# First tile of the first mixing phase read into SBUF within the projection; one identity table for all three phases

## The chip, the cores and the metric

The kernel runs on one core of one Trainium2 chip. The time is the device time of one execution in microseconds (us), from start to end of the program, and the figure used is the median of several executions. Lower is better.

The engines are named as in the profile: PE is the matrix engine (PEld is its weight load), DVE the vector engine, ACT the scalar engine, POOL the general engine, SP the engine that only issues transfers. SPq and ACTq are the transfers that SP and ACT issue; each of the two has a DMA queue of its own (q1 is SP's, q10 is ACT's).

## The reference

One inference step of a two-layer decoder trunk, for a prompt of 2048 tokens and for 8 samples of 8 tokens, width 1024, all in float32:

```
for l in range(2):
    mod = silu(c) @ w_ada[l] + b_ada[l];  shift, scale, gate = split(mod, 3)
    h = rms_norm(x, g_pre[l]) * (1 + scale) + shift
    y, states = mixer_ab(h, ...) if l == 0 else mixer_c(h, ...)
    x = x + gate * rms_norm(y, g_post[l])

mixer_ab: gq,gk,gv,gz,glr, rq,rk,rv,rz = split(h @ w_in)      # 3088 columns
    log_a = log_sigmoid(glr @ w_gate_up + b_gate) / 16        # 4 gated heads
    q_r, k_r = rotary(rq), rotary(rk)                         # 4 retention heads
    o, S = chunked_gated_linear_attn(q, k, v, log_g, s0)      # S_t = g_t S_{t-1} + k_t v_t
    y = (normalised per head(o) * silu(z)) @ w_out
mixer_c:  a gated delta rule with a width-4 convolution on q, k, v
```

## The kernel before

The program is four phases, one after the other. Each phase is a block with one instruction list per engine, and the engines meet at a barrier where a phase ends (`Phase.end`). Between phases, large intermediate results go through DRAM.

1. **inab** (`phase_in_ab`, the first 658 us): the product `h @ w_in` of layer 0. The tokens are taken in four blocks of 512 and a fifth with the 64 sample tokens. Each float32 product is three half-precision matmuls (line 613). Before it, layer 0's conditioning (`Cond`) is computed, with the weight `w_ada`, and the first block is normalised and transposed with the identity table. q and k leave to the DRAM array `qk0`, v to `v0`, z to `z0` and the decays to `dec0`.
2. **mixab** (`phase_mix_ab`, to about 1059 us): the recurrence over 16 tiles of 128 tokens and then the samples. A tile on PE is: transpose k with the identity (line 1675), scores (1685), outputs (1696, 1700), key-values (1709), then the output projection (1117). DVE masks the scores with the table `incl` (1540), decays the state (1549), takes statistics (1557) and gates.
3. **inc** (`phase_in_c`): layer 1's input projection, whose first instructions on PE transpose the convolution weights, which SP has loaded as rows (line 1872), with the identity (2141).
4. **mixc** (`phase_mix_c`): layer 1's recurrence. The change doesn't touch it.

What sets the order around the change:

- **Tables.** Constants (identity, masks, selectors, decays) stand side by side in one DRAM array, in the order `TABLE_ORDER`. `load_tables` (line 172) issues one transfer for each name. Phase inab loads three (`ident`, `sel`, `sel_s`) as SP's third to fifth transfers and seven more after the `w_ada` loads; mixab loads seven; inc loads three. The tables of a phase are in that phase's own SBUF, so the identity is loaded again in each.
- **Waits on tables.** PE's list begins with a wait for them in inab (`first_in`, line 1010), in mixab (`tab_in`, line 1668) and in inc (line 2136); in mixab and inc it is for all tables of the phase. DVE's list in mixab begins with the same wait (1529) and one for POOL's memsets (`init`, 1530, signalled by line 1439, the last of five).
- **Tiles in mixab.** SP's list loads tile 0 (four transfers: q and k, v, z, decays; lines 1370 to 1374), then the tables, then tile 1, then the residual rows of two tiles, the gate, two gain vectors `gn` and `cT`. The rooms for tiles are two of each, used in turn; tile 2 is loaded into the first (`turn(0, ...)`, line 1405) once tile 0 has been mixed.
- **Operand rooms in inab.** The normalised input of a block of 512 tokens stands in one of two rooms of 128 partitions by 4096 floats. Blocks 1 and 3 use the room `h` of phase inab; the fifth block uses a room in `y`. So `h` is not read after block 3. In mixab and inc a room of the same size, `raw_next`, is allocated outside the phases; mixab writes it only near its end.
- **SP in inab's last part.** SP stores a block's results as they come (`outputs`). Between block 3's stores and those of the fifth block it issues the load of rotation angles for the latter (`rot_load`, line 774). The phase ends when the last stores of v and z have landed (line 785).

Of the kernel before, what the change touches and what calls it, by code (L numbers as in the profile page):

```python
# [23 lines left out]
P = 128  # L24
# [165 lines left out]
def width(names):  # L190
    return sum(TABLE[n][1] for n in names)
# [426 lines left out]
def phase_in_ab(nc, io, modT, seq):  # L618
# [9 lines left out]
    first_names = ["ident", "sel", "sel_s"]  # L628
    names = ["swap", "reset", "reset_s", "dec", "dec_s", "retd", "retd_s"]
    tab = ph.sb("tab", [P, width(first_names + names)])  # L630
    tv = table_views(tab, first_names + names)
# [41 lines left out]
    prep = Prep(nc, ph, 0, io["x_prompt"], io["x_sample"], modT, tv["ident"], nt, pst, io["keep32"])  # L673
# [35 lines left out]
    def _(sp):  # L709
        sp.dma_start(c9[0:1, :], io["c_prompt"]).then_inc(c_in, 16)  # L710
        sp.dma_start(c9[1:C9, :], io["c_sample"]).then_inc(c_in, 16)
        load_tables(sp, first_in, tab, first_names, io["table"])
# [5 lines left out]
        load_tables(sp, tab_in, tab[:, width(first_names):], names, io["table"])  # L718
# [205 lines left out]
    def _(dve):  # L924
# [13 lines left out]
        dve.wait_ge(tab_in, 16 * len(names))  # L938
# [70 lines left out]
    def _(pe):  # L1009
        pe.wait_ge(first_in, 16 * len(first_names))  # L1010
# [11 lines left out]
        pe.wait_ge(tab_in, 16 * len(names))  # L1022
# [269 lines left out]
def phase_mix_ab(nc, io, seq):  # L1292
# [4 lines left out]
    io["raw_next"] = io["keep"].enter_context(nc.sbuf_tensor("raw_next", [P, KT, BLK], F32))  # L1297
# [4 lines left out]
    tv = table_views(tab, names)  # L1302
# [4 lines left out]
    dec = [ph.sb(f"dec{i}", [P, 8]) for i in range(2)]  # L1307
    ktok = ph.sb("ktok", [P, PAIRS, P])
# [14 lines left out]
    tile_in = [s("tile_in0"), s("tile_in1")]  # L1323
    init, within = s("init"), s("within")
# [54 lines left out]
    def _(sp):  # L1379
        load_tile(sp, 0, 0, P)  # L1380
# [7 lines left out]
        sp.dma_start(cT[:].rearrange("p k c -> p (k c)"), io["cT"]).then_inc(cT_in, 16)  # L1388

# [15 lines left out]
        turn(0, 0, 0, P, P)  # L1405
# [122 lines left out]
    def _(dve):  # L1528
        dve.wait_ge(tab_in, 16 * len(names))
# [77 lines left out]
        for t in range(4):  # L1607
# [3 lines left out]
            tile(t, t % 2, t // 2)  # L1611
# [55 lines left out]
    def _(pe):  # L1667
        pe.wait_ge(tab_in, 16 * len(names))
# [65 lines left out]
        for t in range(2):  # L1734
            tile(t, t, 0)
# [65 lines left out]
def phase_in_c(nc, io, modT, seq):  # L1801
# [3 lines left out]
    names = ["ident", "incl", "incl_s"]  # L1805
    tab = ph.sb("tab", [P, width(names)])
    tv = table_views(tab, names)
# [327 lines left out]
    def _(pe):  # L2135
        pe.wait_ge(tab_in, 16 * len(names))
# [93 lines left out]

        pe.wait_ge(g_ready, 1)
# [1076 lines left out]
```

## Time and profile before

| | |
|---|---|
| median of 3 runs | 2683.37 us (2681.66 to 2688.16) |
| the profiled execution | 2690.28 us, its span 2688.5 us |
| PE busy | 2488.4 us, 93% of the span |
| DVE, ACT, POOL busy | 49%, 35%, 30% |
| mean granted clock of PE | 0.966 |

The span runs from the first to the last instruction of one execution, taken by the hardware profiler; all positions below are in us from its start. A granted clock of 1.00 is 2.4 GHz, one of 0.50 is 1.2 GHz. A timeline row shows start, duration, engine, line, operation, tiles written and read, how many instructions it merges, and in brackets how long the engine had been idle before it and what released it. For a row that merges several instructions the duration reaches from the first to the last.

### The profile page before, as it was taken

How to read it: one execution, taken by the hardware profiler on the slowest of the kernel's cores; microseconds unless marked ns; L12 is line 12 of the kernel's file. 1: busy time of each engine (PE TensorE's matmuls, PEld its weight loads, DVE VectorE, ACT ScalarE, POOL GpSimd, SP SyncE). 2: the span in 40 equal slices, each digit the busy share in tenths (PEclk: the TensorE clock that was granted, in tenths of full speed). 3: DMA queues.
4: the chain of work that ended last, by engine and by line, in shares of the span. 5: the costliest groups of instructions: out<-in, count | busy, mean ns of one | idle time of the engine just before them, and what ended most of it. 6: DMA issues, size and time to landing. Idle time of an engine off the chain costs nothing. (4 is left out here: it accounts for less than half of the span.)

```text
span 2688.5 us, 53779 instructions
## 1 busy us (share of the span) xinstructions
PE 2488.4 (93%) x20987; PEld 1504.2 (56%) x21052; DVE 1321.5 (49%) x2927; ACT 929.0 (35%) x2666; POOL 798.8 (30%) x848
## 2 busy tenths in 40 slices
PE   6999999997899986998999999994899999999998
PEld 2444444444555542443444444454788787887876
DVE  3412121110678853891652626523666666665666
ACT  3533241312111113442331322233545454454541
POOL 2531011011111112552000000005555646565564
PEclk9999999998899996998999999996999999999998
DMA  8441211123454544552121211117512223131213
GB/s 292 137 153 44 86 48 71 44 96 111 175 178 144 178 134 135 151 159 80 63 71 44 71 58 46 55 36 191 135 57 89 80 78 91 58 111 57 80 45 91
DMA packets 256585, 270.37 MB, mean 101 GB/s; under 512 B 31223, under 2 KB 189959, under 8 KB 256378
## 3 DMA queue, kind: packets, MB, share of 16 engines
q1 hardware_dynamic: 184858, 217.28, 24.8%
q10 hardware_dynamic: 71520, 50.13, 6.6%
q8 instruction: 155, 2.54, 0.4%
q14 instruction: 52, 0.43, 0.1%
HBM read 180.00 MB, written 87.36 MB: 99 GB/s over the span
## 5 line engine op out<-in xcount | busy, mean ns | idle before, releaser
L613 PE MATMUL inc_b<-raw_next,inc_w_hi 128*128 128x512 f16 (+1 forms) x760 | 228.3, 381 | 2.1 <-ACT inc_taps L1963 0.9
L613 PE MATMUL inc_b<-keep,inc_w_hi 128*128 128x512 bf16 (+1 forms) x762 | 227.1, 379 | 1.4 <-ACT inc_ub L1982 0.2
L613 PE MATMUL inab_b<-inab_wt,keep 128*128 128x512 f16 x768 | 167.1, 379 | 4.3 <-POOL inab_wt L562 4.1
L613 PE MATMUL inab_b<-inab_wt,inab_h 128*128 128x512 f16 x768 | 166.4, 379 | 0.0
L1117 PE MATMUL mixab_y<-keep,mixab_oT_hi 128*128 128x512 f16 x512 | 153.3, 381 | 8.4 <-DVE mixab_f_y L1197 6.7
L2075 DVE SCALAR_TENSOR_TENSOR inc_acc<-inc_ub,inc_taps,inc_acc 128x512 f32<-128x512 f32 x192 | 152.0, 792 | 6.8
L2071 DVE COPY inc_ub<-inc_halo 128x3 f32<-128x3 f32 x96 | 21.4, 223 | 253.8 <-ACT inc_ub L1982 253.8
L1982 ACT ACTIVATE inc_ub<-inc_b 128x512 f32<-128x512 f32 x96 | 57.2, 595 | 254.0 <-PE inc_b L613 249.7
L613 PE MATMUL inc_b<-raw_next,inc_w_lo 128*128 128x512 bf16 x368 | 140.4, 382 | 0.0
L613 PE MATMUL inc_b<-keep,inc_w_lo 128*128 128x512 bf16 x366 | 138.7, 379 | 0.0
L877 ACT ACTIVATE inab_vz<-inab_b 128x512 f32<-128x512 f32 (+1 forms) x68 | 40.6, 596 | 254.4 <-PE inab_b L613 242.8
L613 PEld LDWEIGHTS inab_b<-inab_wt,keep 128*128 128x128 bf16 (+1 forms) x768 | 74.9, 98 | 95.5 <-issue 6.0
L613 PEld LDWEIGHTS inc_b<-raw_next,inc_w_hi 128*128 128x128 f16 x768 | 75.4, 98 | 90.6 <-issue 2.2
L613 PEld LDWEIGHTS inab_b<-inab_wt,inab_h 128*128 128x128 bf16 (+1 forms) x768 | 75.1, 98 | 90.8 <-issue 1.1
L613 PEld LDWEIGHTS inc_b<-keep,inc_w_hi 128*128 128x128 f16 x768 | 74.9, 98 | 89.3
L398 DVE TENSOR_SCALAR keep<-keep,inab_rstd 128x1024 f32<-128x1024 f32 (+1 forms) x13 | 12.1, 932 | 201.9 <-POOL inab_rstd L393 201.9
L2466 POOL TENSOR_TENSOR mixc_levels<-mixc_BT,mixc_tab 128x512 f32<-128x512 f32 (+1 forms) x82 | 110.1, 1374 | 1.5 <-DVE mixc_BT L2760 1.5
L562 POOL TENSOR_TENSOR inc_w_lo<-inc_stage,inc_w_hi 128x1024 f16<-128x1024 f32 (+1 forms) x33 | 78.0, 2363 | 84.2 <-ACT inc_w_hi L556 84.2
L613 PE MATMUL inc_b<-inc_w_hi,raw_next 128*128 128x512 f16 (+2 forms) x400 | 85.8, 313 | 16.6 <-POOL inc_w_lo L562 16.6
L525 POOL TENSOR_TENSOR keep<-keep 128x1024 f16<-128x1024 f32 x12 | 27.7, 2309 | 240.1 <-ACT keep L520 240.1
L1117 PE MATMUL mixc_y<-mixc_w_hi,mixc_oT_hi 128*128 128x512 f16 x256 | 97.4, 380 | 0.0
L1117 PE MATMUL mixab_y<-keep,mixab_oT_lo 128*128 128x512 f16 x256 | 97.3, 380 | 0.0
(523 smaller groups left out, 6128.8 us busy)
## 6 DMA issues: line engine op xcount, KB each, us to landing
tmp_qkv<-inc_so SPq DMA_DIRECT2D x96, 256.0 KB, 2.0
mixc_qkv<-tmp_qkv SPq DMA_DIRECT2D x15, 1536.0 KB, 7.7
inc_stage<-in_w_in_c ACTq DMA_DIRECT2D x32, 512.0 KB, 4.6
inab_stage<-in_w_in_ab ACTq DMA_DIRECT2D x24, 512.0 KB, 4.1
mixab_cw<-in_w_ada ACTq DMA_DIRECT2D x6, 2048.0 KB, 14.7
inab_wt<-in_w_ada SPq DMA_DIRECT2D x10, 1024.0 KB, 14.9
keep<-in_x_prompt SPq DMA_DIRECT2D x16, 512.0 KB, 4.0
tmp_v<-inab_vz SPq DMA_DIRECT2D x32, 256.0 KB, 3.8
```

Of the source, the lines that this page charges most:

```text
L398: dve.tensor_scalar(self.xn[0:n, :], self.x[par][0:n, :], self.rs[0:n, par:par + 1], None, ALU.mult).then_inc(self.xnd, 1)
L525: pool.tensor_tensor(room[1][:, :, col:col + n], self.hf[:, :, 0:n], room[0][:, :, col:col + n], ALU.subtract).then_inc(self.lo_done, 1)
L562: eng.tensor_tensor(self.place(1, c0, m), self.stage[u % self.slots][:, :, 0:m], self.place(0, c0, m), ALU.subtract).then_inc(self.lo_done, 1)
L613: last = nc.tensor.matmul(dst, lhs(a, k), rhs(b, k), start=(k == 0 and i == 0), stop=(k == KT - 1 and i == len(PASSES) - 1))
L877: act.activation(vz[0:rows, j % 4, :], src[0:rows, :], ACT.Copy if i < 2 else ACT.Silu).then_inc(evac, 1)
L1117: last = self.nc.tensor.matmul(self.banks[half][0:n, :], (self.oT_hi, self.oT_lo)[a][:, h, 0:n], self.w[b][:, h, half * 512:(half + 1) * 512],
L1982: act.activation(ub[g % 2][:, CONV - 1:], src[:], ACT.Copy).then_inc(evac, 1)
L2071: chain.link(dve.tensor_copy(u_[:, 0:CONV - 1], h_))
L2075: chain.link(dve.scalar_tensor_tensor(a_v, win(i), taps[:, c, i:i + 1], a_v, ALU.mult, ALU.add))
L2466: pool.tensor_tensor(BTm[w][0:n], BT[0:n, :, 0:HB], bc(tv[f"pick{w}"][0:n].unsqueeze(1), [n, H, HB]), ALU.mult).then_inc(btm_ready, 1)
```

## The change

- The room `raw_next` is allocated from inab on, and serves there as the room `h`. After block 3's last product SP loads the first tile of mixab into it (12 KB for each partition and 8 floats), between the load of rotation angles and the fifth block's stores, and waits for it at the phase's end.
- In mixab tile 0 is read from this room, as a third set of rooms (index 2). SP's list there begins by adding 64 to `tile_in[0]`, in place of tile 0's load. Tile 2 is loaded as the last of the transfers at the start, with no wait, and `turn(0, ...)` is gone.
- The three first tables are in the order `sel`, `sel_s`, `ident`, in a tile that is kept through inab, mixab and inc. mixab and inc don't load them again. PE's waits for tables at the start of mixab and inc are gone (inc's stands before the matmuls with `incl` near its end).
- `load_tables` joins names that are neighbours in the DRAM array: inab's first tables are one transfer, its seven others one, mixab's four remaining ones two, inc's two remaining ones one.

```diff
 def load_tables(eng, sem, dst, names, table_d):
     at = 0
+    for c0, w in runs(names):
+        eng.dma_start(dst[:, at:at + w], table_d[:, c0:c0 + w]).then_inc(sem, 16)
+        at += w
+
+def runs(names):
+    out = []
     for n in names:
         c0, w = TABLE[n]
-        eng.dma_start(dst[:, at:at + w], table_d[:, c0:c0 + w]).then_inc(sem, 16)
-        at += w
+        if out and sum(out[-1]) == c0:
+            out[-1] = (out[-1][0], out[-1][1] + w)
+        else:
+            out.append((c0, w))
+    return out
...
-    first_names = ["ident", "sel", "sel_s"]
+    first_names = ["sel", "sel_s", "ident"]
     names = ["swap", "reset", "reset_s", "dec", "dec_s", "retd", "retd_s"]
...
+    tab0 = io["keep"].enter_context(nc.sbuf_tensor("tab0", [P, width(first_names)], F32))
+    raw_next = io["raw_next"] = io["keep"].enter_context(nc.sbuf_tensor("raw_next", [P, KT, BLK], F32))
+    tab = ph.sb("tab", [P, width(names)])
...
+    pre = [raw_flat[:, i * D:(i + 1) * D] for i in range(3)] + [raw_flat[:, 3 * D:3 * D + 8]]
+    io["first_tile"] = pre
...
         rot_load(nb, NS)
+        sp.wait_ge(mm, G * nb)
+        for i in range(4):
+            sp.wait_ge(vz_out[i], 16 + 16 * TPB)
+        sp.dma_start(pre[0].rearrange("p (g n) -> p g n", g=8), io["qk0"][:, :, 0:P].rearrange("g p n -> p g n")).then_inc(pre_in, 16)
+        sp.dma_start(pre[1], io["v0"][0:P, :]).then_inc(pre_in, 16)
+        sp.dma_start(pre[2], io["z0"][0:P, :]).then_inc(pre_in, 16)
+        sp.dma_start(pre[3], io["dec0"][:, 0, :]).then_inc(pre_in, 16)
         outputs(nb, NS, 1, [])
+        sp.wait_ge(pre_in, 64)
...
-    names = ["ident", "incl", "incl_s", "seq", "sel", "sel_s", "eye_h"]
+    names = ["incl", "incl_s", "seq", "eye_h"]
...
+    for room, a, g in zip((qk, v, z), io["first_tile"], (8, H, H)):
+        room.append(a.rearrange("p (g n) -> p g n", g=g))
+    dec.append(io["first_tile"][3])
...
+    tile_in.append(tile_in[0])
...
     def _(sp):
-        load_tile(sp, 0, 0, P)
+        sp.sem_inc(tile_in[0], 64)
         load_tables(sp, tab_in, tab, names, io["table"])
         load_tile(sp, 1, 1, P)
...
         sp.dma_start(cT[:].rearrange("p k c -> p (k c)"), io["cT"]).then_inc(cT_in, 16)
+        load_tile(sp, 2, 0, P)
...
-        turn(0, 0, 0, P, P)
...
-            tile(t, t % 2, t // 2)
+            tile(t, t % 2 if t else 2, t // 2)
...
-        pe.wait_ge(tab_in, 16 * len(names))
...
-            tile(t, t, 0)
+            tile(t, (2, 1)[t], 0)
...
-    names = ["ident", "incl", "incl_s"]
+    names = ["incl", "incl_s"]
...
-        pe.wait_ge(tab_in, 16 * len(names))
...
+        pe.wait_ge(tab_in, 16 * len(runs(names)))
         pe.wait_ge(g_ready, 1)
```

## Rows read from the trace of the kernel before

**Rows 1.** The page, slices: busy tenths of PE and its granted clock

```profile
PE   6999999997899986998999999994899999999998
PEclk9999999998899996998999999996999999999998
```

**Rows 2.** Timeline around the end of inab (tile view for the first row)

```profile
L767 SPq DMA_DIRECT2D tmp_z<-inab_vz x6: 332/333/467, 603.7 to 654.6; - x6
...
658.32 0.38 SPq L1370 DMA_DIRECT2D mixab_qk<-tmp_qk  x1
...
660.32 3.37 SPq L177 DMA_DIRECT2D mixab_tab<-in_table  x7
661.26 0.52 POOL L1439 MEMSET mixab_S<- 128x512 f32 x1
...
667.29 1.11 PE L1675 MATMUL mixab_kv<-mixab_tab,mixab_qk 128*128 128x128 f32 x4 [13.38 <-DMA mixab_tab<-in_table]
...
670.49 1.12 DVE L1540 TENSOR_TENSOR mixab_sc<-mixab_be,mixab_tab 64x512 f32<-64x512 f32 x2 [35.59 <-PE mixab_bo L1685]
```

**Rows 3.** Transfers issued from 655 to 700: count, KB each, us to landing

```profile
mixab_tab<-in_table SPq DMA_DIRECT2D x4, 64.0 KB, 4.5
```

**Rows 4.** Transfers issued from 0 to 4

```profile
inab_tab<-in_table SPq DMA_DIRECT2D x2, 64.0 KB, 1.9
```

**Rows 5.** Timeline of mixab's first tile, and of a later one (last two rows)

```profile
673.62 0.77 PE L1696 MATMUL mixab_oe<-mixab_v,mixab_sc 128*128 128x128 f32 x2 [3.31 <-DVE mixab_S L1549]
...
679.05 1.09 PE L1709 MATMUL mixab_kv<-mixab_v,mixab_ktok 128*64 128x128 f32 x16
...
710.29 0.39 PE L1696 MATMUL mixab_oe<-mixab_v,mixab_sc 128*128 128x128 f32 x2
...
713.27 1.09 PE L1709 MATMUL mixab_kv<-mixab_v,mixab_ktok 128*64 128x128 f32 x16
```

**Rows 6.** Stretches: length; busy us of PE, PEld, DVE, ACT, POOL; granted clock, DMA, GB/s

```profile
45.00:48.00 3.00, 3.00 (x10) 0.55 (x8) 0.00 (x0) 0.00 (x0) 0.00 (x0) 0.63 1.09 371
...
630.00:634.00 4.00, 3.63 (x14) 2.30 (x15) 2.38 (x4) 2.01 (x8) 2.12 (x1) 0.62 0.57 168
...
658.00:662.00 4.00, 0.00 (x0) 0.00 (x0) 0.00 (x0) 0.00 (x0) 3.44 (x5) 0.53 0.63 171
...
678.00:680.00 2.00, 2.00 (x30) 1.78 (x28) 0.83 (x5) 0.00 (x0) 0.00 (x0) 0.82 0.00 0
...
900.00:920.00 20.00, 19.52 (x183) 12.25 (x181) 15.54 (x46) 4.31 (x10) 4.17 (x6) 1.00 0.51 170
```

**Rows 7.** Timeline of SP and PE in inab's last part

```profile
619.64 0.56 SPq L774 DMA_DIRECT2D inab_cs<-in_rot  x1
...
630.37 1.43 PE L1058 MATMUL inab_b<-inab_r,inab_tab 128*128 128x64 f32 x8 [4.57 <-ACT inab_r L869]
...
630.67 0.38 SPq L747 DMA_DIRECT2D tmp_qk<-inab_u  x1
```

**Rows 8.** Timeline of the program's start

```profile
1.50 1.31 SPq L177 DMA_DIRECT2D inab_tab<-in_table  x3
...
6.58 1.06 ACT L373 ACTIVATE keep<-keep 128x1024 f32<-128x1024 f32 x1 [0.60 <-DMA keep<-in_x_prompt]
...
34.79 9.14 SPq L177 DMA_DIRECT2D inab_tab<-in_table  x7
...
48.76 1.06 ACT L556 ACTIVATE inab_wc_hi<-inab_stage 128x1024 f16<-128x1024 f32 x1 [6.71 <-DMA inab_stage<-in_w_in_ab]
```

**Rows 9.** Timeline around the start of inc

```profile
1063.96 1.61 SPq L177 DMA_DIRECT2D inc_tab<-in_table  x3
...
1068.86 2.12 POOL L562 TENSOR_TENSOR inc_w_lo<-inc_stage,inc_w_hi 128x1024 f16<-128x1024 f32 x1 [5.32 <-ACT inc_w_hi L556]
...
1070.65 1.12 PE L2141 MATMUL inc_t<-inc_tab,inc_so 4*128 4x4 f32 x13 [14.42 <-DMA inc_so<-in_conv_c]
...
1073.41 0.63 PE L613 MATMUL inc_b<-raw_next,inc_w_hi 128*128 128x512 f16 x1 [0.87 <-ACT inc_taps L1963]
```

More of the change, by code:

```diff
@@ L627, in phase_in_ab @@
     nb, nt = seq // BLK, seq // P
-    first_names = ["ident", "sel", "sel_s"]
+    first_names = ["sel", "sel_s", "ident"]
     names = ["swap", "reset", "reset_s", "dec", "dec_s", "retd", "retd_s"]
-    tab = ph.sb("tab", [P, width(first_names + names)])
-    tv = table_views(tab, first_names + names)
+    tab0 = io["keep"].enter_context(nc.sbuf_tensor("tab0", [P, width(first_names)], F32))
+    raw_next = io["raw_next"] = io["keep"].enter_context(nc.sbuf_tensor("raw_next", [P, KT, BLK], F32))
+    tab = ph.sb("tab", [P, width(names)])
+    tv = {**table_views(tab0, first_names), **table_views(tab, names)}
+    io["first_tables"] = table_views(tab0, first_names)
+    raw_flat = raw_next[:].rearrange("p k n -> p (k n)")
+    pre = [raw_flat[:, i * D:(i + 1) * D] for i in range(3)] + [raw_flat[:, 3 * D:3 * D + 8]]
+    io["first_tile"] = pre
+    pre_in = ph.sem("pre_in")
     wgu = ph.sb("wgu", [16, 2 * P])
@@ L672, in phase_in_ab @@
     act_chain, dve_chain = ph.sem("act_chain"), ph.sem("dve_chain")
-    prep = Prep(nc, ph, 0, io["x_prompt"], io["x_sample"], modT, tv["ident"], nt, pst, io["keep32"])
+    prep = Prep(nc, ph, 0, io["x_prompt"], io["x_sample"], modT, tv["ident"], nt, pst, io["keep32"], raw_next)
     prep.rooms += [None] * (nb - 2) + [[y[:, e, BLK // 2:BLK].bitcast(dt).rearrange("p (k n) -> p k n", k=KT)
@@ L711, in _ @@
         sp.dma_start(c9[1:C9, :], io["c_sample"]).then_inc(c_in, 16)
-        load_tables(sp, first_in, tab, first_names, io["table"])
+        load_tables(sp, first_in, tab0, first_names, io["table"])
         for t in range(TPB):
@@ L717, in _ @@
         cond.load_halves(sp, 2)
-        load_tables(sp, tab_in, tab[:, width(first_names):], names, io["table"])
+        load_tables(sp, tab_in, tab, names, io["table"])
         sp.dma_start(wgu[:], io["w_gla_gate_up"]).then_inc(small_in, 16)
@@ L937, in _ @@
             cond.add(dve, n)
-        dve.wait_ge(tab_in, 16 * len(names))
+        dve.wait_ge(tab_in, 16 * len(runs(names)))
         for g in range(2):
@@ L1009, in _ @@
     def _(pe):
-        pe.wait_ge(first_in, 16 * len(first_names))
+        pe.wait_ge(first_in, 16 * len(runs(first_names)))
         pe.wait_ge(silu, 1)
@@ L1528, in _ @@
     def _(dve):
-        dve.wait_ge(tab_in, 16 * len(names))
+        dve.wait_ge(tab_in, 16 * len(runs(names)))
         dve.wait_ge(init, 1)
@@ L1804, in phase_in_c @@
     nb, nt = seq // BLK, seq // P
-    names = ["ident", "incl", "incl_s"]
+    names = ["incl", "incl_s"]
     tab = ph.sb("tab", [P, width(names)])
-    tv = table_views(tab, names)
+    tv = {**io["first_tables"], **table_views(tab, names)}
     UNITS = [(i * P, min(P, N_C - i * P)) for i in range((N_C + P - 1) // P)]
@@ L2135, in _ @@
     def _(pe):
-        pe.wait_ge(tab_in, 16 * len(names))
         ident = tv["ident"]
@@ L2229, in _ @@
         turned(2)
+        pe.wait_ge(tab_in, 16 * len(runs(names)))
         pe.wait_ge(g_ready, 1)
```

3 lines of the change are left out of this document (1 added, 2 removed).

## The prediction

> **What bounds the kernel now.** I read the page's slices first: PE is busy in nine tenths or more of nearly every slice and its granted clock is full, with a few dips [rows 1]. So the time is PE's work plus the places where PE stands still or runs at the low clock level, and a change that leaves its matmuls as they are can only work on those places. One dip is at 655 to 690, the seam between inab and mixab. Then I read the timeline there. PE's next instruction after inab is at 667.29, after 13.38 us of idleness that a table's landing ended, so its last one of inab ended at 653.9. The last store of z is issued at 654.6, and the barrier is over at 658.3, when SP issues its first transfer of mixab [rows 2]. The same timeline gives the two smaller places: the program's start, where SP's loads run as one stream, and the start of inc, where PE waited for the rows of convolution weights, loaded behind three tables [rows 8, 9]. The transfer views gave the landing times, and the view by stretches the clock [rows 3, 4, 6].
>
> **The seam inab to mixab.** Before: tile 0's four loads are issued from 658.32, the seven tables from 660.32 to 663.69, and PE begins at 667.29. DVE masks the first scores at 670.49, so transposes and scores take 3.20 us [rows 2]. After, PE waits only for SP's addition to `tile_in[0]`, its first instruction, and starts at about 658.5; I take 0.2 us for the release. Scores are then done at 658.5 + 3.2 = 661.7.
>
> DVE's mask now waits for three things. (a) Scores: 661.7. (b) `init`: POOL's last memset runs from 661.26 for 0.52 us, so 661.8 [rows 2]; it starts right after the barrier, and nothing in it moves. (c) `incl`, in the first of two table transfers, the second of which counts too. An issue took 3.37/7 = 0.48 us [rows 2], so the second is issued by 659.3. For its landing the bounds are 1.9 us, the landing of a table on a quiet queue at the program's start [rows 4], and 4.5 us, that of a table behind tile 0's 1.5 MB in this seam [rows 3]. That is 660.7 to 663.3, if the time to land is counted from an issue at 658.8. Nothing stands ahead of the tables any more, so it is the quiet row that resembles them: I take 1.9. The mask then starts at 661.85 in place of 670.49: **8.64 us earlier**. With the late landing it would be 663.4, or 7.1 us earlier.
>
> From the mask on, tile 0 runs as before: mask and state decay on DVE, outputs and key-values on PE, statistics, gate. All of its operands (room 2, its decays) have been in SBUF since the projection. Tile 1's loads are issued right behind two tables instead of seven, by about 661.8, and PE turns to tile 1 only after tile 0's key-values, which end at 679.05 + 1.09 = 680.1 before [rows 5] and at 671.5 after. So 9.7 us are there to land 1.5 MB, which need 4 us at the 371 GB/s of a saturated stretch [rows 6]. Tile 2's loads move from a wait on tile 0 to the end of the opening list, at about 666 to 668, and are needed a tile later; I cost them at nothing, with the mixing of tiles 0 and 1 as cover. Without that cover PE would wait for those 4 us. Behind tile 1 the residual rows, the gate and the gains come as before and earlier by about the same. The loop's tiles depend on each other and not on the clock on the wall, so the shift passes to the phase's end.
>
> **Where the first tile's loads go.** SP issues them after the load of rotation angles at 619.64; its waits are for block 3's last product, which is done, since that block's stores stand ahead in SP's list, and for the stores of block 0. Four issues at 0.48 us end at about 622.2, and SP's next transfer in the old order is q's store at 630.67 [rows 7], so no store is behind them. The 1.5 MB need 4 us of the DMA engines and are in by 627, in a stretch where PE itself stands idle until 630.37 [rows 7], and the new wait at the phase's end is long met. Cost nothing; if they were in the way of something on PE's path it would be at most those 4 us.
>
> **The program's start.** Three table transfers become one: SP's issues take 1.31 us for three [rows 8], 0.44 each, so all of SP's later loads are issued 0.87 us earlier. ACT's first square is released by the landing of the first x tile at 6.58 [rows 8], and ACT's conversion of the second weight unit at 48.76 by a landing too, behind the `w_ada` stream; the first product waits behind both. So the stream sets the pace from end to end, and it moves by **0.87 us**. The seven tables behind it become one transfer of the same 0.75 MB. Here is a cost that I can only bound: it is under way about when ACT's weight unit lands. At 371 GB/s it takes 2.0 us [rows 6], and if it held up the unit by all of that, the start would be 1.1 us later than before rather than 0.87 earlier. I take no delay, since `w_ada`'s 2 MB pieces are ahead of both and the unit has nearly landed when the tables' turn comes.
>
> **The start of inc.** Three tables, 1.61 us, become one of about 0.5 us, so the convolution rows are issued **1.1 us** earlier; PE's transposes at 1070.65 were released by them. The next gate is near: POOL's low half of the first weight unit ends at 1070.98, while PE's first product is at 1073.41 [rows 9], and it needs both. The transposes and ACT's copy behind them stay, so all 1.1 us pass, and at most 2.4 could. The least is 0, if it is the weight loads on the other queue that decide when the rows land.
>
> **The sum.** 8.64 + 0.87 + 1.1 = 10.6 us, so the profiled execution's 2690.28 becomes 2679.7. That execution was 6.9 us above the median of the runs, 2683.37; the three seams are waits, which I take to be the same in both. **2683.4 - 10.6 = 2672.8 us.** A measurement of this kernel tells about 0.3% from no change, 8.05 us, so the line between faster and same is at 2675.3.
>
> **Rivals.**
>
> *The clock lifts earlier (gain 13.2, 2670.2).* In this seam PE was at the low level (1.2 GHz) from just after 658 and came back to 2.4 GHz within 678 to 680 [rows 6]. Tile 0's outputs, 673.62 to 679.05, took 5.43 us; a later tile's, at 2.4 GHz, 713.27 - 710.29 = 2.98 us [rows 5]. The idle stretch before them shrinks from 13.4 to 4.5 us. In a like case, an idle stretch of 4.57 us that ended at 630.37 [rows 7], the 4 us from 630 have a mean of 0.62, so PE was at the low level for some 3 us and then at full level [rows 6]. If the scores lift it here too, and the wait for the mask (3.2 us) doesn't drop it, 2.5 us more are gained. Against it: scores of 3 us did not lift it before. The Trainium skill ("TensorE: Matmul & The Clock Gate", section on the HAM clock gate) says that the gate watches in windows that run free of the kernel, so the same work can meet either level. By that rule the trace's one case of each sort is what one would see.
>
> *Tables land late (gain 9.1, 2674.3).* The two transfers land as in the old seam, at 663.3. For it: the tables' landing in this very seam took 4.5 us; against it: they had tile 0 ahead of them. 10.6 less 1.5 us is 9.1.
>
> *The start is given back (gain 7.5, 2676).* The merged table delays ACT's weight unit by up to 2.0 us: 10.6 - 2.0 = 8.6, and with inc's 1.1 hidden behind the weights 7.5, 2675.9; I name the case by 2676. For it: the DMA engines are saturated there, and the landing of that unit is what ACT waits 6.71 us for [rows 8]. The Trainium skill ("DMA: Bandwidth & Descriptors", "Queues, rings and completion order") says that a DMA engine takes turns between queues packet by packet. By that rule SP's queue with 5.9 KB pieces would leave ACT's 512-byte ones a smaller share than with the small tables. No row of before shows it.
>
> *It doesn't do what it says (gain 2, 2681).* Something else of the seam, such as an instruction list that starts late, keeps PE until 667. Against it: SP and POOL were both running within 0.1 us of 658.3 [rows 2].
>
> *Slower: the clock in mixab's loop.* The changed rhythm could leave PE at the low level in the tiles that follow. In the loop PE is busy 19.52 of 20 us at full level [rows 6], so each us of that work run at 1.2 GHz costs one more. From 10.9 us of it on, some 21 us of time, the kernel is slower than before; twice that, one slice's work of 19.5 us, gives 2692. For it: the dips in the slices are of that length [rows 1]. Against it: at 19.52 of 20 us PE has no wait in the loop, and the dips stand where it waits.
>
> **Chances.** Forecast 0.58, clock lifts 0.14, tables late 0.12, start given back 0.09, not done 0.03, slower 0.04. The likeliest gives 2672.8. The three runs before span 6.5 us, so I allow a median some 2 us either way. The range reaches to 2666.5 (clock lifted, inc at its most, and the spread) and to 2679 (start given back, and the spread). Faster: most of the first two, and of the third two in three, 0.77; same 0.19; slower 0.04.
>
> **What would show it.** PE's first matmul of mixab at 658.5 less 0.9, released by nothing of a table; the first mask 3.3 us later with POOL's memset as the releaser; no loads of tile 0 after the barrier, and four at 620; the first square of the start 0.9 us earlier; inc's transposes 1.1 us earlier relative to the barrier. It is wrong if the mask waits for `mixab_tab`, if PE stands in tile 1 or 2 for a tile's landing, or if the tiles of the loop are spaced otherwise than before.

## The result and the profile after

| | before | after |
|---|---|---|
| median, 5 runs each on one chip | 2687.0 us (2681.66 to 2689.9) | 2671.03 us (2669.06 to 2671.28) |
| the profiled execution, its span | 2690.28, 2688.5 us | 2671.11, 2669.3 us |
| mean granted clock of PE | 0.966 | 0.969 |

The ratio is 0.9944 with a 95% interval of 0.9932 to 0.9956: 15 us faster (11.8 to 18.3). Forecast were 10.6 us and 2672.8; the two profiled spans lie 19.2 us apart. The medians differ by 16.0 us. What has to be explained is the seam, which came as forecast, and the 4 to 5 us beyond the sum of 10.6.

The seam first, on the timeline of the kernel after (start, duration, engine, line; in brackets idle time and releaser), against [rows 2, 5, 7]:

```profile
618.75 0.56 SPq L792 DMA_DIRECT2D inab_cs<-in_rot  x1
619.49 2.09 SPq L805 DMA_DIRECT2D raw_next<-tmp_qk  x1
621.63 0.58 SPq L806 DMA_DIRECT2D raw_next<-tmp_v  x1
622.25 0.43 SPq L807 DMA_DIRECT2D raw_next<-tmp_z  x1
622.73 0.66 SPq L808 DMA_DIRECT2D raw_next<-tmp_dec  x1
629.78 0.39 SPq L765 DMA_DIRECT2D tmp_qk<-inab_u  x1
...
657.74 1.12 PE L1703 MATMUL mixab_kv<-tab,raw_next 128*128 128x128 f32 x4 [4.73 <-SPq L1409]
657.77 0.84 SPq L176 DMA_DIRECT2D mixab_tab<-in_table  x2
...
660.61 0.52 POOL L1468 MEMSET mixab_S<- 128x512 f32 x1
661.23 1.12 DVE L1569 TENSOR_TENSOR mixab_sc<-mixab_be,mixab_tab 64x512 f32<-64x512 f32 x2 [27.22 <-POOL mixab_S L1468]
...
664.36 0.77 PE L1724 MATMUL mixab_oe<-raw_next,mixab_sc 128*128 128x128 f32 x2 [3.60 <-DVE mixab_S L1578]
668.88 1.09 PE L1737 MATMUL mixab_kv<-raw_next,mixab_ktok 128*64 128x128 f32 x16
```

PE is idle for 4.73 us at the seam in place of 13.38 [rows 2], released by SP's addition to `tile_in[0]`. The mask starts 3.49 us behind PE's first transpose and is released by POOL's memset. No load of tile 0 stands behind the barrier; its four stand at 619.5 to 623.4. They landed 6.7 to 7.6 us after their issue, the last at 630.1, just behind the issue of the next store at 629.78; PE needs the tile only at 657.74. The row of the transfers issued between 657.5 and 664 (count, KB, us to landing) answers to [rows 3, 4]:

```profile
mixab_tab<-in_table SPq DMA_DIRECT2D x1, 128.0 KB, 2.1
mixab_tab<-in_table SPq DMA_DIRECT2D x1, 36.0 KB, 2.0
```

So the tables land in 2.0 to 2.1 us, as on the quiet queue of [rows 4] and not as behind 1.5 MB [rows 3].

Of the clock, the stretches of the kernel after (length; busy us of PE, PEld, DVE, ACT, POOL; granted clock, DMA, GB/s), against [rows 6]:

```profile
658.00:660.00 2.00, 2.00 (x32) 1.67 (x33) 0.00 (x0) 0.60 (x1) 2.00 (x3) 0.50 0.42 98
661.00:664.00 3.00, 0.00 (x0) 0.00 (x0) 2.70 (x5) 0.00 (x0) 0.13 (x1) 1.00 1.08 380
664.50:667.00 2.50, 2.50 (x12) 2.50 (x13) 0.00 (x0) 0.00 (x0) 0.00 (x0) 0.50 1.04 404
667.00:669.00 2.00, 2.00 (x24) 1.76 (x24) 0.00 (x1) 0.00 (x0) 0.00 (x0) 0.89 0.87 320
900.00:920.00 20.00, 19.52 (x154) 11.70 (x153) 16.22 (x58) 3.13 (x7) 2.89 (x6) 1.00 0.87 262
```

The scores still run at 1.2 GHz (0.50). Behind them the full level is granted (1.00), but just while PE stands idle for the mask. The first outputs run at 1.2 GHz again, and PE returns to 2.4 GHz between 667 and 669, still inside the outputs: from L1724 to L1737 it takes 4.52 us, where it took 5.43 [rows 5]. The loop is as before, 19.52 of 20 us at full level.

Start and inc, against [rows 8, 9]:

```profile
1.49 0.36 SPq L176 DMA_DIRECT2D tab<-in_table  x1
5.72 1.06 ACT L384 ACTIVATE keep<-keep 128x1024 f32<-128x1024 f32 x1 [0.18 <-DMA keep<-in_x_prompt]
33.99 3.94 SPq L176 DMA_DIRECT2D inab_tab<-in_table  x1
48.48 1.06 ACT L567 ACTIVATE inab_wc_hi<-inab_stage 128x1024 f16<-128x1024 f32 x1 [6.79 <-DMA inab_stage<-in_w_in_ab]
...
1041.31 1.11 SPq L1174 DMA_DIRECT2D tmp_x_s<-mixab_f_x  x2
1046.16 0.35 SPq L176 DMA_DIRECT2D inc_tab<-in_table  x1
1046.56 1.35 SPq L1900 DMA_DIRECT2D inc_so<-in_conv_c  x3
1052.79 1.14 PE L2168 MATMUL inc_t<-tab,inc_so 4*128 4x4 f32 x13 [13.89 <-DMA inc_so<-in_conv_c]
1055.17 1.03 PE L624 MATMUL inc_b<-raw_next,inc_w_hi 128*128 128x512 bf16 x2 [0.47 <-ACT inc_taps L1991]
```

ACT's first square is 0.86 us earlier than before, but the weight unit only 0.28. In inc the rows are issued 0.40 us after SP's first transfer there instead of 1.66 (1065.62 in the trace before), yet PE's transposes come 6.63 us after that transfer where they came 6.69 [rows 9]: behind their own issue the rows took 6.23 us, where they took 5.03.

### The profile page after: what moved, and what is told of

It reads as the page before. It is cut to its first block and busy times, and to the rows that moved or that the text cites. A ratio compares the mean times of both kernels' runs of the same rounds, so it can differ in the third digit from the quotient of the medians.

```text
span 2669.3 us, 53829 instructions
## 1 busy us (share of the span) xinstructions
PE 2490.4 (93%) x21052; PEld 1502.1 (56%) x21052; DVE 1321.3 (50%) x2927; ACT 929.5 (35%) x2666; POOL 793.8 (30%) x848
## 5 line engine op out<-in xcount | busy, mean ns | idle before, releaser
L624 PE MATMUL inc_b<-raw_next,inc_w_hi 128*128 128x512 bf16 (+1 forms) x768 | 230.3, 382 | 0.5 <-ACT inc_taps L1991 0.5
L624 PE MATMUL inab_b<-inab_wt,raw_next 128*128 128x512 f16 x768 | 166.4, 379 | 0.0
L624 PE MATMUL inc_b<-raw_next,inc_w_lo 128*128 128x512 bf16 x384 | 146.4, 381 | 0.0
L624 PE MATMUL inc_b<-keep,inc_w_lo 128*128 128x512 bf16 x384 | 145.5, 379 | 0.0
L624 PEld LDWEIGHTS inab_b<-inab_wt,raw_next 128*128 128x128 bf16 (+1 forms) x768 | 75.1, 98 | 90.9 <-issue 1.1
L536 POOL TENSOR_TENSOR raw_next<-keep,raw_next 128x1024 f16<-128x1024 f32 (+1 forms) x13 | 29.4, 2264 | 284.0 <-ACT raw_next L531 284.0
## 6 DMA issues: line engine op xcount, KB each, us to landing
mixab_cw<-in_w_ada ACTq DMA_DIRECT2D x6, 2048.0 KB, 14.5
```

The source lines that it names most:

```text
L536: pool.tensor_tensor(room[1][:, :, col:col + n], self.hf[:, :, 0:n], room[0][:, :, col:col + n], ALU.subtract).then_inc(self.lo_done, 1)
L624: last = nc.tensor.matmul(dst, lhs(a, k), rhs(b, k), start=(k == 0 and i == 0), stop=(k == KT - 1 and i == len(PASSES) - 1))
```

## The experiments

Times are ratios to the kernel before, run on the same chip, in us of its 2686. Because single executions of one kernel span up to 13 us, most conclusions rest on stretches of the traces. They are given here for every run. "Seam": PE idle. "0-2", "3-5": spacing of DVE's state decay between those tiles. "Tail": from the last tile's decay to the last store of x_s. "inc": from there to the transposes. "Unit": ACT's conversion of [rows 8], from the start. All read from the traces' timelines.

| run | seam | 0-2 | 3-5 | tail | inc | unit | gain (95%), us |
|---|---|---|---|---|---|---|---|
| before | 13.38 | 34.28 | 41.74 | 117.29 | 12.00 | 48.76 | |
| before_again | 12.99 | 32.89 | 40.45 | 115.21 | 11.79 | 48.56 | |
| start_only | 13.54 | 34.10 | 41.30 | 116.52 | 11.81 | 48.20 | -0.3 (-2.7 to 1.9) |
| port_before | 12.90 | 33.13 | 40.15 | 112.26 | 11.98 | 48.68 | 3.8 (1.3 to 6.2) |
| after | 4.73 | 32.91 | 38.31 | 114.01 | 11.48 | 48.48 | 15.0 (11.8 to 18.3) |
| repeat | 4.72 | 33.15 | 41.42 | 113.41 | 11.71 | 48.33 | 14.2 (11.0 to 17.5) |
| port_after | 4.73 | 33.07 | 41.42 | 112.56 | 11.35 | 47.93 | 14.5 (11.0 to 17.7) |
| inc_old | 4.72 | 33.01 | 38.34 | 113.83 | 11.92 | 49.33 | 8.3 (5.1 to 11.5) |
| late_tile | 11.81 | 33.25 | 41.04 | 112.97 | 11.50 | 48.36 | 5.6 (3.2 to 8.1) |
| table_wait | 9.40 | 33.05 | 39.71 | 113.00 | 11.81 | 47.28 | 5.4 (3.0 to 7.8) |
| undone | 12.60 | 32.90 | 38.18 | 113.30 | 11.98 | 48.58 | -0.8 (-3.2 to 1.6) |
| spread | 4.72 | 33.15 | 34.34 | 112.51 | 11.80 | 48.37 | 21.0 (17.2 to 24.7) |
| small | 4.73 | 33.34 | 39.17 | 112.04 | 9.14 | 49.28 | 15.0 (11.3 to 18.5) |
| all_three | 4.73 | 33.16 | 34.34 | 112.08 | 9.04 | 49.18 | 21.0 (17.2 to 25.0) |

### The same kernel once more

> The changed kernel once more, unaltered. The parts priced ahead add up to 10.6 us, the medians say 16.0 us (2687.0 against 2671.0). Theory A, chance: part of the 16 is the scatter of the kernel before (its runs span 8.2 us), so this pair comes out between 10 and 13 us. Theory B, something systematic follows from the change that was not priced: 15 to 17 us again.

Measured: 2672.91 us, ratio 0.9947. Neither theory came whole: the gain is 12.8 us by the medians, inside theory A's range, and 14.2 by the ratio, with an interval of 11.0 to 17.5 that holds most of A's range and all of B's. That more than 10.6 follows is borne out by both pairs together, by a margin that isn't well known. Also, this profiled execution took 2679.5 in its span, 10.2 more than the first one of the same kernel. 5.3 us of that are in inab (PE starts mixab at 663.08 in place of 657.74, of the same instructions) and 3.1 in the tiles 3 to 5. So the 19.2 us between the first two traces were partly a lucky draw.

### The two halves of the seam

```diff
 # late_tile
-        sp.wait_ge(mm, G * nb)
-        for i in range(4):
-            sp.wait_ge(vz_out[i], 16 + 16 * TPB)
-        sp.dma_start(pre[0].rearrange("p (g n) -> p g n", g=8), io["qk0"][:, :, 0:P].rearrange("g p n -> p g n")).then_inc(pre_in, 16)
...
         sp.sem_inc(tile_in[0], 64)
+        load_tile(sp, 0, 2, P)
         load_tables(sp, tab_in, tab, names, io["table"])
```

> The changed kernel, but tile 0 is loaded at the start of mixab again, ahead of the two table transfers; identity kept, PE waits for no table. Theory A, each of the two parts of the seam removes only what the other leaves: PE's first transpose waits for tile 0's last transfer, issued at about 659.2 and landing 5.6 us later (the decays' row of before), so it starts at about 664.5 in place of 657.7, the mask stands at 667.7 in place of 661.2, and the kernel is 6 to 6.5 us slower than the changed one. Rival: the tables were all that PE waited for and tile 0's landing is nearly free (PE 660 to 661, 0 to 2 us slower than the changed one).

```diff
 # table_wait
-        load_tables(sp, tab_in, tab, names, io["table"])
+        for n, dst in tv.items():
+            c0, w = TABLE[n]
+            sp.dma_start(dst, io["table"][:, c0:c0 + w]).then_inc(tab_in, 16)
...
     def _(pe):
+        pe.wait_ge(tab_in, 16 * 7)
```

> The changed kernel, but in mixab seven table transfers are issued one by one, the identity among them, and PE waits for all, as before; tile 0 is read early as in the changed kernel. Theory A, tables with nothing ahead of them land fast: seven issues of 0.48 us end at 661.1, landing 1.9 us, so PE starts at 663.1, the mask at 666.3 in place of 661.2: 5 us slower than the changed kernel. Rival, a table takes 4.5 us to land in this seam whatever is ahead of it: PE at 665.6, the mask at 668.8, 7.6 us slower.

PE's first instruction of mixab in late_tile, then in table_wait:

```profile
660.09 0.42 SPq L1395 DMA_DIRECT2D raw_next<-tmp_dec  x1
...
665.86 1.11 PE L1696 MATMUL mixab_kv<-tab,raw_next 128*128 128x128 f32 x4 [11.81 <-DMA raw_next<-tmp_dec]
```

```profile
661.56 1.86 SPq L1412 DMA_DIRECT2D mixab_tab<-in_table  x4
...
664.86 1.12 PE L1706 MATMUL mixab_kv<-tab,raw_next 128*128 128x128 f32 x4 [9.40 <-DMA mixab_tab<-in_table]
```

Late tile: PE waits 7.1 us longer than in the changed kernel, theory A, a little more than expected (the decays landed 5.8 us after their issue, which stood 1.65 behind SP's first). Table wait: 4.7 us longer, theory A: the last of seven issues ends at 663.42 and PE runs 1.44 us later. So with either wait left in, more than half of the 8.65 us is still lost: the two waits lay side by side. By PE's idle time, reading the tile early alone saves 4.0 us, dropping the wait for tables alone 1.6, both together 8.65. The ratios say 9 us slower than the changed kernel in both cases, more than the traces show at the seam.

### The start alone

```diff
-    first_names = ["ident", "sel", "sel_s"]
+    first_names = ["sel", "sel_s", "ident"]
...
-        load_tables(sp, first_in, tab, first_names, io["table"])
+        load_joined(sp, first_in, tab[:, 0:width(first_names)], first_names, io["table"])
...
-        load_tables(sp, tab_in, tab[:, width(first_names):], names, io["table"])
+        load_joined(sp, tab_in, tab[:, width(first_names):], names, io["table"])
```

> The kernel before, with inab's first three tables in one transfer and its seven others in one; all else as before. Theory A: 0.9 us faster than before, as the spans of the two traces show between their starts and 619. Rival 1, the 0.75 MB transfer delays the weight unit: up to 1.1 us slower. Rival 2, the missing 5 us of the sum come from here, through a shift of everything later against the clock: 3 us or more faster.

Measured: no difference, and rival 2 is out; the interval (2.7 us slower to 1.9 faster) holds theory A's 0.9 us and rival 1's 1.1 alike. The column "unit" shows more than the ratio can: 48.56 to 48.76 in four traces with separate tables (mean 48.65), 47.28 to 49.33 in ten traces with joined ones, mean 48.47. SP's stream moves by 0.9 us, but what waits for ACT's queue does so by 0.2 on average, and in three of ten traces it came later than before.

### Where the rest came from: DVE and POOL in mixab's tail

PE's start in mixab to inc's first product took 406.1, 401.2 and 404.6 us in the three traces of the old order, and 397.4, 400.8, 399.2 and 397.8 in the four with the whole change in mixab, a mean of 5.1 less, behind the seam. The largest part is in the tail, by the table 116.3 against 113.5. (The undone kernel, below, takes 396.7 us here and yet is as slow as the one before, so this stretch of a single execution does not stand for the median.) Here is what differs, in before_again (its timeline; POOL, DVE, ACT, PE):

```profile
1021.13 1.27 POOL L1229 TENSOR_SCALAR mixab_e_ms<-mixab_e_ss 128x1 f32<-128x1 f32 x1 [6.14 <-ACT mixab_exn L1225]
1022.49 2.46 POOL L1231 TENSOR_TENSOR mixab_e_rs<-mixab_e_ms,mixab_f_mhalf 128x1 f32<-128x1 f32 x1
...
1021.13 1.23 DVE L1653 TENSOR_TENSOR mixab_Ss<-mixab_Ss,mixab_dec_s 128x1024 f32<-128x1024 f32 x1
1022.27 2.28 DVE L1621 TENSOR_TENSOR mixab_vm<-mixab_v,mixab_tab 64x2048 f32<-64x2048 f32 x1
...
1024.98 1.15 ACT L1235 ACTIVATE mixab_exn<-mixab_v,mixab_e_rs 128x1024 f32<-128x1024 f32 x1 [4.05 <-POOL mixab_e_rs L1231]
...
1026.18 0.66 PE L1241 MATMUL mixab_be<-mixab_tab,mixab_exn 128*128 128x128 f32 x4 [2.88 <-ACT mixab_exn L1235]
```

POOL's two instructions on one column, otherwise 0.19 and 0.54 us, are as long as the two DVE instructions beside them, each of which reads two SBUF operands. ACT and PE wait for the second. The Trainium skill ("SBUF — State Buffer", section "SBUF: two separate sides") says that DVE with two SBUF inputs and a GpSimd instruction that reads SBUF share a port pair which whoever starts first keeps for its whole instruction. The rows agree where DVE starts first. Where POOL is ahead, as in this trace of repeat, it takes 0.19 us beside DVE's addition, which reads PSUM, and then 0.54:

```profile
1015.65 1.29 DVE L1680 TENSOR_TENSOR mixab_Ss<-mixab_Ss,mixab_kv 128x512 f32<-128x512 f32 x2 [6.39 <-PE mixab_kv L1814]
1016.69 0.19 POOL L1255 TENSOR_SCALAR mixab_e_ms<-mixab_e_ss 128x1 f32<-128x1 f32 x1 [5.96 <-ACT mixab_exn L1251]
1016.96 0.54 POOL L1257 TENSOR_TENSOR mixab_e_rs<-mixab_e_ms,mixab_f_mhalf 128x1 f32<-128x1 f32 x1
1016.97 1.25 DVE L1682 TENSOR_TENSOR mixab_Ss<-mixab_Ss,mixab_dec_s 128x1024 f32<-128x1024 f32 x1
```

But DVE's multiplication, which starts 0.01 us behind POOL's 0.54, is not held for that instruction: it takes 1.25 us, where it takes 1.22 or 1.23 in before, before_again and port_before. In this direction the measurement decides against the page's rule.

> The kernel before, unaltered, for a second profile of it. Between mixab's last state decay and the last store of x_s its trace and that of start_only show 117.3 and 116.5 us, the four kernels with the change 113.0 to 114.0: in the two old ones a POOL instruction on one column (normally 0.19 us) takes 1.2 and the next (0.54) takes 2.5, both beside a DVE multiplication of two SBUF operands; ACT and then PE wait for it. Theory A, this is a collision that the old kernel runs into each time: again 116.5 or more, with POOL at 1.2 and 2.5. Theory B, it is chance: about 113.5, with POOL at 0.19 and 0.54.

Theory A held, with 115.2 rather than 116.5: POOL 1.27 and 2.46. The clock differs too: in the trace of before PE runs at 1.2 GHz for 20.5 us from 1026.9 on, right at its stall, and here for 13.6 us from 1032.0 on.

```diff
             chain.link(last)
+            if p == 1:
+                dve.wait_ge(early.rsd, 3)
             dve.tensor_tensor(Ss[p][:], Ss[p][:], bc(dec_s[:, p, :].unsqueeze(2), [P, NSEQ, DV]), ALU.mult).then_inc(state_ready, 1)
```

> The kernel before with one wait more: in mixab's tail DVE holds its multiplication of the second pair's sample states until POOL has computed the third early reciprocal root. Theory A, POOL is held up by DVE instructions that read two SBUF operands, and PE waits for it: POOL's two instructions take 0.2 and 0.55 us, PE's transposes wait under 1 us in place of 2.9, the low clock behind them goes too, the stretch from the last state decay to the last store of x_s falls by 2 to 3.5 us, and so does the time against before. Rival, POOL was late by itself (its instructions are as long without DVE): nothing changes or it becomes slower by up to 2 us, since DVE now waits.

Its trace:

```profile
1019.48 0.19 POOL L1229 TENSOR_SCALAR mixab_e_ms<-mixab_e_ss 128x1 f32<-128x1 f32 x1 [6.20 <-ACT mixab_exn L1225]
1019.75 0.54 POOL L1231 TENSOR_TENSOR mixab_e_rs<-mixab_e_ms,mixab_f_mhalf 128x1 f32<-128x1 f32 x1
...
1020.40 1.23 DVE L1655 TENSOR_TENSOR mixab_Ss<-mixab_Ss,mixab_dec_s 128x1024 f32<-128x1024 f32 x1 [0.96 <-POOL mixab_e_rs L1231]
...
1021.57 0.66 PE L1241 MATMUL mixab_be<-mixab_tab,mixab_exn 128*128 128x128 f32 x4
```

Theory A: DVE waits 0.96 us, PE's wait is gone, the tail is 3 to 5 us shorter than in the three old traces and the kernel 3.8 us faster. The cause of this stall is shown. PE's stretch at 1.2 GHz, which was expected to go, did not: it lasts 13.6 us, from 1027.4 on.

The same wait in the changed kernel:

> The changed kernel with port_before's wait alone. Theory A, in the changed kernel POOL is ahead of DVE by 0.02 to 0.8 us each time (six traces), so the wait finds its condition met or all but met: 0 to 1 us faster or slower than the changed kernel, where the same wait took 3.8 us (1.3 to 6.2) from the kernel before. Then the collision accounts for most of what the sum of 10.6 us left out. Theory B, the collision is chance in both kernels and the profiles merely caught it so: 1.5 to 3 us faster than the changed kernel.

Measured 0.9946: the wait that took 3.8 us from the old kernel takes nothing measurable from the new one (gain 14.5 us, against 15.0 and 14.2 without it). With an interval of some 3 us either way on each of these, theory B's 1.5 to 3 us can't be excluded. And the trace goes against theory A's condition:

```profile
1012.74 1.29 DVE L1680 TENSOR_TENSOR mixab_Ss<-mixab_Ss,mixab_kv 128x512 f32<-128x512 f32 x2 [6.72 <-PE mixab_kv L1816]
1014.07 0.19 POOL L1255 TENSOR_SCALAR mixab_e_ms<-mixab_e_ss 128x1 f32<-128x1 f32 x1 [6.14 <-ACT mixab_exn L1251]
1014.98 1.23 DVE L1684 TENSOR_TENSOR mixab_Ss<-mixab_Ss,mixab_dec_s 128x1024 f32<-128x1024 f32 x1 [0.96 <-POOL mixab_e_rs L1257]
```

DVE waits 0.96 us for POOL, as in port_before. POOL starts 1.33 us behind DVE's addition, as in the traces of the old order (1.32 to 1.37), where DVE's multiplication started 1.32 behind its addition and held POOL up. So this execution of the changed kernel stood where the old ones did, and only the added wait kept it from the stall. In the other nine traces of the changed kernel and its variants POOL is 0.02 to 0.88 us ahead of the multiplication. The old kernel's traces have the stall each time (three of three, with port_before at the same place), the changed kernel's more rarely, but nothing in the change rules it out. Joining the start's tables did not bring this about (start_only has the stall).

In undone all priced parts go back at once; it has the edits of late_tile, table_wait and inc_old (below), and no table is joined to its neighbour:

```diff
-        if out and sum(out[-1]) == c0:
+        if False:
```

> The changed kernel with all priced parts undone at once: every table transfer on its own, tile 0 loaded after the barrier, PE waiting for seven tables in mixab and three in inc. What stays of the change: the kept identity and room and with them the places in SBUF, the third room for tile 0, tile 2's load in the opening list. Theory A, POOL's collision in mixab's tail hangs on the timing of transfers that these parts don't touch, and is missed by all nine kernels with the new places while the three runs with the old ones had it: the collision stays away (POOL 0.19 and 0.54, tail 113 us) and the kernel is 2 to 5 us faster than before. Theory B, what misses it is chance or a consequence of the priced parts: POOL 1.2 and 2.5, tail 115 to 117 us, and within 1 us of before.

Neither theory came whole. The time is that of the kernel before, to within 0.12%, so the priced parts together carry the full 15 us. But its profiled execution has no full stall: POOL's first instruction, 0.07 us ahead of DVE's multiplication, took 0.19 us and the second 1.42 in place of 2.46, and the tail 113.30. This finish is decided by less than 0.1 us, and one execution doesn't tell how the others went. What shifts it between the kernels stays open, and with it a part of the sizes: late_tile and table_wait lose some 2 and 4 to 5 us more against the changed kernel than PE's wait at their seam shows, though their profiled executions have no full stall either.

### The start of inc

```diff
-        load_tables(sp, tab_in, tab, names, io["table"])
+        for n in ("ident", "incl", "incl_s"):
+            c0, w = TABLE[n]
+            sp.dma_start(tv[n], io["table"][:, c0:c0 + w]).then_inc(tab_in, 16)
...
     def _(pe):
+        pe.wait_ge(tab_in, 48)
```

> The changed kernel, but in inc three table transfers (identity, incl, incl_s) stand ahead of the convolution rows again and PE waits for them. Theory A, the rows' landing is set by the weight loads of the other queue: PE's transposes come 11.9 us behind the last store of x_s in place of 11.5 to 11.8, 0.2 us, and the time is the changed kernel's. Rival (the prediction's term), 1.1 us: the transposes come 12.8 us behind that store.

In the trace theory A: 11.92 us from the store to the transposes, beside 11.35 to 11.71 in three traces of the changed kernel's inc with the same mixab (11.50 to 11.81 in late_tile, table_wait and spread), so some 0.3 to 0.4 us and not 1.1. The time is another matter: 2678.19, some 6 us slower than the changed kernel. Nothing in its trace shows this: inab to its last matmul is 657.3 us (653.0 and 658.4 in after and repeat), mixab from PE's start to inc's first product is 397.8 us (397.4 and 400.8), inc to mixc 749.4 (749.1 and 749.5), and the rest 865.2 (865.0 and 866.1). That excess stays unexplained. It matters for the whole account: inc_old's only edit stands behind mixab's tail, and its excess is at least as large as the 4 to 5 us for which the stall is the candidate.

```diff
-        pool.memset(vm_room[1][:], 0.0)
         pool.memset(S[:], 0.0).then_inc(init, 1)
+        pool.memset(vm_room[1][:], 0.0).then_inc(init, 1)
...
+        for i in range(3):
+            sp.dma_start(rows[32 * i:32 * i + CONV, :], io["conv_c"][:, i * D:(i + 1) * D]).then_inc(rows_in, 16)
         prep.first_tiles_done(sp)
         load_tables(sp, tab_in, tab, names, io["table"])
-        for i in range(3):
-            sp.dma_start(rows[32 * i:32 * i + CONV, :], io["conv_c"][:, i * D:(i + 1) * D]).then_inc(rows_in, 16)
```

> The changed kernel with two changes of order: POOL clears the state ahead of vm in mixab and signals then, and in inc SP loads the convolution rows ahead of everything else. Theory A, the gates are the memset (mask at 3.49 us behind PE's start, scores ready at 3.2) and the issue of the rows: mask 0.3 us earlier, PE's transposes of inc 0.9 us earlier against the barrier, 1.2 us together, too little for the ratio to tell. Rival for inc, the weight loads of the other queue decide when the rows land: transposes no earlier than now against the barrier (8.0 us behind the end of the last phase in the changed kernel).

Its trace:

```profile
1042.75 1.11 SPq L1174 DMA_DIRECT2D tmp_x_s<-mixab_f_x  x2
1046.90 0.96 SPq L1899 DMA_DIRECT2D inc_so<-in_conv_c  x3
1051.89 1.15 PE L2169 MATMUL inc_t<-tab,inc_so 4*128 4x4 f32 x13 [11.56 <-DMA inc_so<-in_conv_c]
1053.17 2.12 POOL L573 TENSOR_TENSOR inc_w_lo<-inc_stage,inc_w_hi 128x1024 f16<-128x1024 f32 x1 [5.51 <-ACT inc_w_hi L567]
```

The mask came 0.3 us earlier, as expected (3.19 behind PE's start). PE's transposes came 9.14 us after the store, 2.2 to 2.6 earlier and not 0.9: the rows are issued 1.1 us earlier against the store, and they land 5.0 us after their issue in place of 6.2 with the joined table ahead of them. The rival (transposes no earlier, since the other queue's weight loads decide) is out. Whether the earlier issue or the missing table shortened the landing, this run doesn't part. But POOL's half of the first weight unit ends at 1055.29, and the product, at 1055.82, waits for it: 3.93 us behind the transposes in place of 2.4 to 2.8. Of 2.4 us about 1.0 is left. The ratio can't tell this from nothing, as said ahead.

### A version that beats both

```diff
-        for n in range(3):
-            cond.load(act, n)
-        with act.Fori(3, nt) as t:
+        for t in range(3, 6):
+            cond.load(act, t - 3)
+            tile(t)
+        with act.Fori(6, nt) as t:
             tile(t)
```

> The changed kernel, but mixab's three w_ada loads (2 MB each) are issued one each ahead of ACT's tiles 3, 4 and 5 instead of all three ahead of tile 3. Tiles 3 to 5 take 38.3 to 41.7 us for two spacings in the six traces, 34.7 without disturbance. Theory A, ACT's 5.2 us of issuing and PE's wait of 3 to 4 us for tile 4's landing come from three loads in a row: with one at a time both go, the two spacings come to 35 us, the kernel is 4 to 6 us faster than the changed one. Rival, each load costs its share wherever it stands (the DMA engines are at 1.05 of their share): 0 to 1 us.

The stretches of tiles 3 to 5 in spread and, below, in repeat:

```profile
722.00:732.00 10.00, 9.70 (x97) 5.73 (x96) 8.81 (x32) 1.18 (x3) 1.91 (x2) 1.00 0.65 224
732.00:742.00 10.00, 9.69 (x80) 6.68 (x78) 7.77 (x14) 1.95 (x4) 0.93 (x3) 1.00 0.97 353
```

```profile
722.00:732.00 10.00, 9.32 (x77) 6.25 (x75) 7.44 (x26) 2.04 (x5) 1.53 (x5) 1.00 1.06 397
732.00:742.00 10.00, 6.12 (x47) 3.35 (x45) 5.99 (x15) 1.28 (x3) 1.31 (x1) 0.66 0.94 355
```

Theory A: with one load at a time PE is busy 9.7 of 10 us in both stretches, at full level; with three in a row it loses 3.6 us of work in the second stretch and the clock falls to 0.66. What PE waits for there is the landing of tile 4, and ACT stands in its third issue (repeat):

```profile
716.03 5.31 ACTq L239 DMA_DIRECT2D mixab_cw<-in_w_ada  x1
...
736.37 1.11 PE L1703 MATMUL mixab_kv<-tab,mixab_qk 128*128 128x128 f32 x4 [3.88 <-DMA mixab_dec<-tmp_dec]
```

In spread both are gone; the run doesn't part them, but only the landing is in PE's way in the rows. Two spacings take 34.34 us in place of 38.2 to 41.7, and the kernel 2666.72 us. By the ratios that is 21.0 us less than before and some 6 less than the changed kernel; the median of small, run beside it on the same chip, is 3.6 us higher.

> The changed kernel with the edits of spread, small and port_before together. In the traces of those three the spread loads took 34.3 in place of 38.3 to 41.4 us in two tile spacings (3.5 to 5 us less after a slower clock), the early rows and the memset order 1.1 and 0.3 us; the wait for POOL took 3 us from a kernel that runs into the collision. Theory A, the collision is missing in the changed kernel anyway: 5 to 6.5 us faster than the changed one, 2665 us or so beside 2671. Theory B, it is there in some executions: 1 to 2 us more.

2667.42 us, ratio 0.9922: 6.0 us less than the changed kernel by the ratios and 3.9 less than port_after, the nearest kernel on the same chip, by the medians. That is theory A's size, and the same as spread alone. The small edits and the wait for POOL add nothing on top that can be measured.

## Why the prediction was right, and where it was not

- **The seam** (8.64): right, mechanism and size. PE idle 4.73 for 13.38, the gates in the order forecast (scores, then the memset); from inab's last matmul to tile 0's state decay 18.9 us became 10.5, 8.4 less. The tables landed in 2.0 to 2.1 us, so the late-landing rival (9.1 in all) is out. Tile 2's load cost nothing, as forecast: PE waits for no landing in tiles 1 and 2 of the trace after.
- **Tile 0's early load** (0): right, with a slower landing than forecast. The four issues took from 619.5 to 623.4 and the last landed at 630.1, not by 627; PE needed the tile 27 us later.
- **The start** (0.87): the step "so the stream sets the pace from end to end" failed. SP's stream and the first square moved by 0.9 us in the first pair. The weight unit, on ACT's queue, moved by 0.2 on average of ten traces. Whether the joined table held it back, as the rival of the start had it, is not shown. The 0.89 us by which the first pair of traces differed at 619 was mostly scatter, and that PE's start at 657.74 met the sign "658.5 less 0.9" was chance: to its last matmul inab took 653.0 to 658.4 us in the fourteen traces, whose instructions there are nearly the same.
- **inc** (1.1): the step "so all 1.1 us pass" failed. The rows were issued 1.26 us sooner after SP's first transfer but took 1.20 us longer to land, so relative to it the transposes moved by 0.06 us in the first pair; the traces of the table say 0.3 to 0.4. Small shows the gate behind: even with the transposes 2.4 us earlier, POOL's weight half holds the gain at 1.0.
- **The clock**: of the rival's two conditions the first held and the second didn't. Behind the scores the granted clock was up (1.00 from 661 to 664), but behind PE's wait for the mask it was down at 0.50 again, so tile 0 gained 0.9 us and not 2.5. Tile 1 lost it: from tile 0's decay to tile 1's it took 16.0 us in place of 16.9 to 17.0 in the two traces of before, and from there to tile 2's 16.9, where before_again had 15.9; undone, with the long seam, has the same 16.0 and 16.9. Over both, the change's traces have 33.0 on average, but so have before_again (32.9) and port_before (33.1), which didn't have the short seam. The 1.4 us there between the first traces are thus no effect of the change. Two readings of the prediction were off without weight: in its like case the low stretch stood from 630.9 to 634.3 with the full level ahead of it, and a slice of [rows 1] is 67.2 us long, not 20.
- **What was left out** (4 to 5 us): in part a stall of POOL beside DVE in mixab's tail, in all three traces of the old order and in full in none of the others, though port_after's would have met it without its wait. Taking it away is worth 3.8 us (1.3 to 6.2) in the kernel before and nothing measurable in the one after. If it were gone from all executions of the changed kernel, the sum would be 8.4 + 0.2 + 0.4 + 3.8 = 12.8, inside the measured 11.8 to 18.3. That it is gone from all is not shown, nor what the change has to do with it: undone lacks the full stall in its trace and is as slow as before. So the 8.4 us of the seam are shown, and the rest of the 15 is in part open. The stretch of tiles 3 to 5 scatters from 38.2 to 41.7 with the change and without it (40.2 to 41.7 in the old order, 38.3 to 41.4 in the new, 38.2 in undone), for a reason that stays open. The prediction took the tail as a thing that only shifts; its view of the slices [rows 1] shows no such thing, but the timeline of the tail would have: 1.22 and 2.46 us on one column.

The total came out right with some luck. The forecast gain of 10.6 us lies outside the measured interval of 11.8 to 18.3; the two failed terms (2.0 us priced, 0.6 there) and the missing one point in opposite directions. That 2671.03 stands only 1.8 us from 2672.8 is due to the starting point: the kernel before was taken at 2683.37, the median of three runs, and its five runs gave 2687.0, 3.6 us more. The range was wide enough since it was made for the clock and for late tables.

## What to carry to other kernels

Two waits that lie side by side are one gate: here leaving either in cost 4.7 or 7.1 of 8.65 us, so price them together and look for the third (the memset, 0.3 us behind the scores). POOL's instructions on one column took 1 to 2.5 us here only when DVE held them up: where one is that long, look at what DVE runs beside it, and put the long operation behind the short one when something on the path waits. A single trace shows or misses such a stall by 0.1 us, so its worth is told by the times of many runs with and without it. Three large loads in a row ahead of a tile's load cost more than the same loads one per tile (4 to 7 us here), though their bytes are the same.

## What the runs showed of the hardware

- A POOL instruction on 128x1 (0.19 or 0.54 us) takes up to 1.27 and 2.46 beside DVE instructions with two SBUF operands (1.23 and 2.28); beside one with a PSUM operand it doesn't.
- The other way round, a DVE instruction that started 0.01 us behind POOL's 0.54 us took 1.25 us in place of 1.22 or 1.23 (repeat).
- ACT stood for 4.9 to 6.8 us in the issue of the third of three 2 MB loads (twelve traces); issued one per tile each took 0.37 to 0.39 us.
- In the changed kernel's seam PE worked on transposes and scores at a granted clock of 0.50, stood idle at 1.00 (661 to 664) and began the outputs at 0.50 again (664.5 to 667).
- The same instruction list of inab took 5.3 us more in one execution than in another (658.4 and 653.0), so a difference of a few us between two single traces can be chance.
